# Gated DeltaNet and sparse-attention block in float32: the sparse heads' norms placed inside the DeltaNet blocks, the top-k search moved to ScalarE, masks made in parts

## The chip, the cores and the metric

The kernel runs on one core of a Trainium2 chip. The metric is the device time of one execution in microseconds (us). Before the change three runs gave 1915.55, 1920.68 and 1921.23 us; their median is 1920.68 us.

## The reference, cut to what matters

One layer over 1024 tokens of width 1024, all in float32. A projection `h @ w_in` feeds two mixers. A is a gated DeltaNet (4 heads of 128, chunks of 64 tokens). B is a sparse attention (8 heads of 64), in which an indexer's score picks 256 keys per query:

```python
dots = einsum('bqhd,bsd->bqhs', qib, ki) * (IDX_HD ** -0.5)
score = einsum('bqh,bqhs->bqs', wib, relu(dots))
score = where(admissible, score, -inf)         # whole chunks of 64, up to the query's own
_, sel = top_k(score, 256)
...
q, k = rms_norm(q per head of 64, g_q), rms_norm(k per head of 64, g_k)
logits = q.k * (DSA_HD ** -0.5) - slopes * abs(qpos - sel)      # only the selected keys
out_B = softmax(logits) @ v
...
S_t = a_t (I - b_t k_t k_t^T) S_{t-1} + b_t k_t v_t^T ;  o_t = S_t^T q_t
out_A = rms_norm(o, g_gdn_out) * silu(z)
x += concat(out_A, out_B) @ w_out ;  x += CrossAttn(...) ;  x += SwiGLU(...)
```

## The kernel before

Every engine has its own program, and semaphores join them; the order of the work is written out by hand. The stages are:

1. Norm of x, the small projections, the indexer: `score` (128 x 4608, eight tiles of 128 queries, tile t with 128(t+1) keys) is summed on VectorE.
2. Projections of the DeltaNet's q, k, v: 12 units of 128 columns (slots u). A unit is 48 matmuls on TensorE (L397 to L399) into one of two pairs of PSUM banks. ScalarE copies it out (L1427, L1428), VectorE makes the causal convolution (L1736, L1738), and ScalarE the silu (L1418).
3. 16 more units (slots v): z, and the sparse heads' q, k, v. ScalarE copies each to `cacc` (L1450) and stores it in DRAM (L1454). Beside them run the squares (L1458) and column sums (L964) of the DeltaNet's q and k, one square root (L1461), and in the last four slots their scaling (L976 on TensorE, L1760 on VectorE).
4. The DeltaNet. `gdn_order` (L571) interleaves, on every engine alike, the 16 parts of `PREP` for block b+1 (four chunks of 64 tokens) with the recurrent scan of the four chunks of block b. A block's triangular inverse takes the parts y1, z1, ... y5, z5: TensorE makes y (L1035), ScalarE copies it to `Ym` (L1484), TensorE makes zt and z (L1035), VectorE subtracts them from `TTm` (L1836) and `Tm` (L1842), and GpSimd prepares the next `gam` (L795). In the text, the body of a block is its y and z parts; its head is what comes before y1 (transposes of k and v, nkbd, kdec, vb, the decays, Am, QKm). TT5 is the last subtraction from TTm; after it follow the w matmuls (L1055). The scan of a chunk: TensorE v (L1070, L1077), ScalarE `vn` (L1528), TensorE L1091 and L1095, VectorE the state `S` (L1854), GpSimd `Sl` (L803).
5. The last four chunks (12 to 15) have no block to prepare beside them. There `dsa` puts the norm of the sparse heads: the stored q and k come back (4 MB), are squared on ScalarE (L1520), summed on TensorE (L1106), a reciprocal of 128x512 is taken (L1889), and for 16 halves of a unit TensorE spreads the factor (L1115) and VectorE scales (L1894). Then the engines meet; TensorE transposes v (L1126) and o (L1135), VectorE makes y (L1906); they meet again.
6. The sparse attention (first logits on TensorE, L1148), the output projection, the cross attention, the feed-forward part.

The top-k is a search on VectorE, 32 rounds for each of the tile pairs (7,2), (6,3), (5,4). A round takes the 8 largest of each row and overwrites them:

```python
dve.max(top8[:, 8 * k:8 * k + 8], score[:, EOFF[t]:EOFF[t + 1]]).then_inc(topk, 1)
dve.match_replace(s, top8[:, 8 * k:8 * k + 8], s, TAKEN).then_inc(topk, 1)
```

The 96 rounds stand, by `top_rounds(n)`, two in each slot u, three in each of 14 slots v, one behind each z part (and behind two parts of the head) in the blocks, and four in stage 5. `logit_bias` (L1868) turns the marked scores into a mask plus distance bias, again in stage 5.

## Time and profile before

| what | value |
| --- | --- |
| median of 3 runs | 1920.68 us |
| the profiled execution's own time | 1923.81 us |
| its span on the core | 1922.1 us |
| busy: TensorE, VectorE, GpSimd, ScalarE | 94%, 55%, 37%, 27% |
| mean granted TensorE clock | 0.965 |
| chain that ended last, by engine | TensorE 76%, VectorE 15%, ScalarE 3%, issue 3% |

Times in the trace count from the span's start. A row of the timeline gives start, length, engine, line, operation, what it writes and reads, and in brackets how long the engine stood idle ahead of it and what ended that. "PEclk" is the granted TensorE clock as a share of 2.4 GHz; 0.50 is the lower of its two levels, 1.2 GHz.

### The profile page before, as it was taken

Reading aid. Unit: us, or ns where it says so; the run is one execution under the profiler, and the core shown is the slowest. Engines: PE = TensorE matmul, PEld = TensorE weight load, DVE = VectorE, ACT = ScalarE, POOL = GpSimd, SP = SyncE. Lnnn points to the kernel's source line nnn. Section 1 sums busy time; section 2 is a strip of 40 time slices with the busy share of each in tenths; the row PEclk is TensorE's granted clock in tenths of the full one; section 3 lists DMA queues with packets and bytes.
Section 4 is the critical chain, followed back from the end, with each engine's and each line's share of the span. In section 5 each row is a group of like instructions: output and inputs, shape, how many; then the busy total and the mean of one; then the engine's idle time right before and its main releaser. Section 6 shows DMA issues by size and latency. Waiting matters only on the chain.

```text
span 1922.1 us, 28223 instructions
## 1 busy us (share of the span) xinstructions
PE 1805.2 (94%) x11097; PEld 1452.5 (76%) x11097; DVE 1059.9 (55%) x1751; ACT 513.1 (27%) x1034; POOL 716.4 (37%) x444
## 2 busy tenths in 40 slices
PE   6999999999977777799999999999999999999999
PEld 5888788777766666356787777788888888888887
DVE  4299889999858778656656347222213221322133
ACT  5366531111111123266504654100110010001000
POOL 4322233333343331056345215434244334443431
PEclk9999999999988888789999999999999999999999
DMA  7221011222220003000221000111111111111112
GB/s 227 74 59 34 23 45 52 69 85 85 94 89 2 2 2 133 12 1 2 88 66 55 23 22 25 53 55 44 44 55 46 53 44 55 44 45 53 44 44 87
DMA packets 112032, 102.42 MB, mean 53 GB/s; under 512 B 5131, under 2 KB 99390, under 8 KB 111678
## 3 DMA queue, kind: packets, MB, share of 16 engines
q1 hardware_dynamic: 109630, 92.67, 15.7%
q10 hardware_dynamic: 2304, 8.39, 1.1%
q8 instruction: 68, 1.11, 0.2%
q14 instruction: 30, 0.25, 0.0%
HBM read 87.42 MB, written 13.63 MB: 53 GB/s over the span
## 4 chain that ended last, share of the span: by engine, by line
PE 76%; DVE 15%; issue 3%; ACT 3%; SPq 1%; POOL 1%; DMA 0%; DVEq 0%; ACTq 0%
PE ps L1317 8%; PE ps L1319 8%; PE ps L1318 8%; PE ps L425 6%; PE ps L426 6%; PE ps L427 6%; PE ps L397 4%; PE ps L398 4%; PE ps L399 4%; DVE top L1723 3%; DVE cacc L1738 2%; DVE score L1727 2%; PE ps L937 2%; PE ps L1148 2%; PE ps L1173 2%
## 5 line engine op out<-in xcount | busy, mean ns | idle before, releaser
L716 POOL TENSOR_TENSOR WS<-WR,zero 128x1024 fp32r<-128x1024 f32 (+1 forms) x119 | 227.9, 1915 | 896.1 <-PE ps L399 314.9
L718 POOL TENSOR_TENSOR WS<-WR,WS 128x1024 fp32r<-128x1024 f32 (+1 forms) x119 | 300.3, 2523 | 9.4
L1317 PE MATMUL ps<-HS,WS 128*128 128x512 f32 x704 | 274.7, 390 | 3.2 <-DVE HS L333 3.2
L1319 PE MATMUL ps<-HS,WS 128*128 128x512 f32 x704 | 274.3, 390 | 0.0
L1318 PE MATMUL ps<-HS,WS 128*128 128x512 f32 x704 | 274.3, 390 | 0.0
L444 DVE TENSOR_TENSOR X<-X,ps 128x512 f32<-128x512 f32 x272 | 184.7, 688 | 155.8 <-PE ps L427 155.8
L2023 DVE TENSOR_TENSOR prod<-sil,ps 128x512 f32<-128x512 f32 x44 | 30.3, 688 | 394.7 <-PE ps L1319 394.7
L397 PE MATMUL ps<-HS,WS 128*128 128x512 f32 (+2 forms) x592 | 228.6, 386 | 7.5 <-ACT raw L1428 3.9
L398 PE MATMUL ps<-HS,WS 128*128 128x512 f32 (+2 forms) x592 | 225.5, 381 | 0.0
L399 PE MATMUL ps<-HS,WS 128*128 128x512 f32 (+2 forms) x592 | 225.1, 380 | 0.0
L1727 DVE MATCH_REPLACE8 score<-top,score 128x1024 f32<-128x1024 f32 (+2 forms) x192 | 166.9, 878 | 0.0
L1723 DVE MAX8 top<-score 128x8 f32<-128x1024 f32 (+2 forms) x192 | 161.3, 882 | 0.0
L1317 PEld LDWEIGHTS ps<-HS,WS 128*128 128x128 f32 x704 | 132.4, 188 | 31.1 <-DVE HS L333 3.8
L1319 PEld LDWEIGHTS ps<-HS,WS 128*128 128x128 f32 x704 | 132.3, 188 | 27.6
L1318 PEld LDWEIGHTS ps<-HS,WS 128*128 128x128 f32 x704 | 132.3, 188 | 27.3
L397 PEld LDWEIGHTS ps<-HS,WS 128*128 128x128 f32 (+1 forms) x592 | 111.8, 189 | 38.4 <-issue 17.2
L426 PE MATMUL ps<-WS,AS 128*128 128x512 f32 x352 | 137.0, 389 | 0.0
L427 PE MATMUL ps<-WS,AS 128*128 128x512 f32 x352 | 136.9, 389 | 0.0
L425 PE MATMUL ps<-WS,AS 128*128 128x512 f32 x352 | 136.9, 389 | 0.0
L1643 ACT ACTIVATE sil<-ps 128x512 f32<-128x512 f32 x44 | 26.4, 599 | 395.0 <-PE ps L1319 395.0
L399 PEld LDWEIGHTS ps<-HS,WS 128*128 128x128 f32 (+1 forms) x592 | 111.7, 189 | 22.1
L398 PEld LDWEIGHTS ps<-HS,WS 128*128 128x128 f32 (+1 forms) x592 | 111.9, 189 | 20.8
(282 smaller groups left out, 2894.5 us busy)
## 6 DMA issues: line engine op xcount, KB each, us to landing
WR<-in_w_gu SPq DMA_DIRECT2D x44, 512.0 KB, 3.8
WR<-in_w_in SPq DMA_DIRECT2D x36, 512.0 KB, 3.7
WR<-in_w_down SPq DMA_DIRECT2D x22, 512.0 KB, 3.6
X<-in_x SPq DMA_DIRECT2D x8, 1024.0 KB, 7.7
dsa_spill<-cacc ACTq DMA_DIRECT2D x12, 512.0 KB, 2.6
KW<-in_w_xkv SPq DMA_DIRECT2D x8, 512.0 KB, 4.9
WR<-in_w_out SPq DMA_DIRECT2D x8, 512.0 KB, 3.5
out<-X SPq DMA_DIRECT2D x8, 512.0 KB, 2.6
```

Of the source, the lines that this page charges most:

```text
L397: pe.matmul(acc, lo, src[:, 0, k, c:c + w], start=(k == 0), stop=False)
L398: pe.matmul(acc, hi, src[:, 1, k, c:c + w], start=False, stop=False)
L399: mm = pe.matmul(acc, hi, src[:, 0, k, c:c + w], start=False, stop=(k == KT - 1))
L425: pe.matmul(acc, xlo, whi, start=(s == 0), stop=False)
L426: pe.matmul(acc, xhi, wlo, start=False, stop=False)
L427: mm = pe.matmul(acc, xhi, whi, start=False, stop=(s == 1))
L716: pool.tensor_tensor(hi, w, bc(zero1[:, 0:1], [P, cols]), ALU.add).then_inc(w_hi, 1)
L718: pool.tensor_tensor(lo, w, hi.bitcast(F32), ALU.subtract).then_inc(w_split, 1)
L1317: pe.matmul(ps[:, b0 + half, :], lo, HS[:, 0, k, c], start=(k == 0), stop=False)
L1318: pe.matmul(ps[:, b0 + half, :], hi, HS[:, 1, k, c], start=False, stop=False)
L1319: mm = pe.matmul(ps[:, b0 + half, :], hi, HS[:, 0, k, c], start=False, stop=(k == KT - 1))
L1723: dve.max(top8[:, 8 * k:8 * k + 8], score[:, EOFF[t]:EOFF[t + 1]]).then_inc(topk, 1)
```

## The change

- **Search.** The 32 bits of each row's 256th largest score are now found one by one. ScalarE makes a Sign of (candidate - score) over a tile with the row sum accumulated (`counts`), VectorE compares three of these sums with a limit and sets or clears the bit (`rank`, three tiny instructions). A half step is three tiles: (7, 2, 3) or (6, 5, 4). 64 half steps: two in each slot u, three in each of the slots v = 0 to 11, four in slot 12. All rounds of max and match_replace are gone.
- **Masks.** From the found threshold VectorE makes each tile's mask (count above, ties, a running sum of the ties, two combinations, the bias); the table `MASKS` and `tail` put the pieces behind parts of the blocks and into the last four chunks.
- **Norms of the sparse heads.** The 4 MB are no longer loaded at once: units of 512 KB are loaded, squared and summed beside the y1 to z4 parts of blocks 0 and 2, loaded again, scaled and stored beside those of blocks 1 and 3 (`beside`; four units each time). The statistics use one PSUM bank; there are two square roots and two reciprocals in place of one. At the end q and k are loaded once more, already scaled.
- **End of the DeltaNet.** v is transposed in chunk 12 and o in chunks 14 and 15 (`tail`), and one meeting of the engines is gone.
- Three weight units are split on GpSimd later (their memory serves the units above).

```diff
-        DSA_PARTS = {0: ("top", 0, 0), 1: ("top", 0, 0), 2: ("on", 0, 0), 3: ("sq", 0, 8), 4: ("sq", 8, 16),
-                     5: ("sd", 0, 0), 6: ("bc", 0, 8), 7: ("bc", 8, 16)}
+        FIRST_HALF, SD_AT = 5, 14
+        def half_of(p):
+            b, i = p // len(PREP), p % len(PREP) - FIRST_HALF
+            return 8 * (b // 2) + i if 0 <= i < 8 else None
...
+            def counts(h, beside):
+                k, g = h // 2, h % 2
+                act.wait_ge(rank_cand, max(1, h))
+                for q in range(3 * g, 3 * g + 3):
+                    t, m = RANKED[q], 6 * k + q
+                    n = (t + 1) * P
+                    if m >= 2:
+                        act.wait_ge(rank_count, m - 1)
+                    act.activation((beside if m % 2 else gB)[:, 0:n], score[:, EOFF[t]:EOFF[t + 1]], ACT.Sign,
+                                   bias=cand[:, q:q + 1].bitcast(F32), scale=-1.0,
+                                   accum_out=count[:, q:q + 1]).then_inc(rank_count, 1)
...
+            def beside(p):                                  # TensorE
+                b, e = p // len(PREP), half_of(p)
+                if e is None:
+                    return
+                g, j = e % 4, e % 8 // 4
+                if b % 2 == 0:
+                    ga.wait(pe, "e1", b)
+                    d0a.wait(pe, f"sq{e}")
+                    d0p.mark(pe.matmul(ps[32 * g:32 * g + 32, 3, :], blkw[:, 30 - 2 * j:62 - 2 * j], sqh[:, e % 2, :],
+                                       start=(j == 0), stop=(j == 1), skip_group_check=True), f"st{e}")
+                else:
+                    ga.wait(pe, "e1", b)
+                    d0d.wait(pe, f"n{e - 1}" if e % 8 else f"rs{b // 2}")
+                    for hp in range(2):
+                        mm = pe.matmul(ps[SD * hp:SD * (hp + 1), 3, :], bc(pick(g, 2 * j + hp), [32, SD]),
+                                       rsH[32 * g:32 * g + 32, :], start=True, stop=True)
+                    d0p.mark(mm, f"bc{e}")
...
-                top_rounds(2)
+                for h in half_steps(u):
+                    rank(h)
...
+            MASKS = {15: [(4, "tie"), (4, "scan"), (4, "out")], 16: [(4, "bias")],
+                     22: [(3, "tie")], 31: [(3, "scan")], 32: [(3, "out"), (3, "bias")],
+                     47: [(5, "tie"), (5, "scan"), (5, "out")], 48: [(5, "bias")],
+                     54: [(2, "tie")], 56: [(2, "scan")], 58: [(2, "out")], 60: [(2, "bias")],
+                     63: [(6, "tie"), (6, "scan"), (6, "out"), (6, "bias")]}
...
+            def tail(h):                                    # VectorE
+                if h == 0:
+                    sp_.wait(dve, "o", 11)
+                    gp.wait(dve, "w1", 3)
+                    mask(7, "tie", tieT, orderT)
+                elif h == 2:
+                    scale_o(0, 0, T_ON)
+                elif h == 3:
+                    mask(7, "scan", tieT, orderT)
+                elif h == 5:
+                    mask(7, "out", tieT, orderT)
+                    dve.wait_ge(z_in, 16)
+                    dve.wait_ge(v_tr, TT)
+                    for t in range(3):
+                        y_of_tile(t)
+                elif h == 7:
+                    mask(7, "bias", tieT, orderT)
+                    for t in range(2):
+                        bias_only(t)
+                    for t in range(3, T_ON):
+                        y_of_tile(t)
```

**TensorE, block 2, parts y1 to z2** (the same in block 0 but for the scan's rows). `gam` and `TTm` make y; `Ym` and `Tm` make zt and z; vn, S are the scan. In the changed program `TTm`, `kdec`, `QKm` and others are slices of `blk`. Before:

```order
L1035 MATMUL ps<-TTm,gam 64x64 x16
L1091 MATMUL ps<-vn,kdec 128x128 x4
L1095 MATMUL ps<-vn,QKm 64x128 x4
L1035 MATMUL ps<-Ym,Tm 64x64 x16
L1035 MATMUL ps<-Tm,Ym 64x64 x16
L1035 MATMUL ps<-TTm,gam 64x64 x16
```

Changed:

```order
L1102 MATMUL ps<-blk,gam 64x64 x16
L1179 MATMUL ps<-sqh,blkw 32x512
L1162 MATMUL ps<-vn,blk 128x128 x4
L1166 MATMUL ps<-vn,blk 64x128 x4
L1102 MATMUL ps<-Ym,Tm 64x64 x16
L1102 MATMUL ps<-Tm,Ym 64x64 x16
L1179 MATMUL ps<-sqh,blkw 32x512
L1102 MATMUL ps<-blk,gam 64x64 x16
```

A column sum (L1179, `sqh` is ScalarE's square) now stands behind each y and each z, ahead of the scan's matmuls and of the next y. In blocks 1 and 3 the two matmuls of a spread factor (`ps<-rsH,ident`) stand in these places.

**VectorE, end of block 0 and begin of block 1.** Before:

```order
L1836 TENSOR_TENSOR TTm<-TTm,ps 128x512
L1723 MAX top_65<-score 128x8 x2
L1727 MATCH_REPLACE score<-top_65,score 128x768
L1727 MATCH_REPLACE score<-top_65,score 128x640
L1802 TENSOR_TENSOR nkbd<-ps,nbed 128x512
```

Changed:

```order
L1997 TENSOR_TENSOR blk<-blk,ps 128x512
L2049 RECIPROCAL rsH<-sdH 128x512
L1851 TENSOR_SCALAR orderW,count<-score,kth 128x640
L1873 TENSOR_SCALAR count<-count 128x1
L1874 TENSOR_SCALAR tieW<-score,kth 128x640
L1876 SCALAR_TENSOR_TENSOR orderW<-ones_61,tieW 128x640
L1878 SCALAR_TENSOR_TENSOR tieW<-orderW,count,tieW 128x640
L1879 SCALAR_TENSOR_TENSOR tieW<-score,kth,tieW 128x640
L1967 TENSOR_TENSOR nkbd<-ps,nbed 128x512
```

Between the block's last subtraction and the first product of the next block a reciprocal and six mask instructions have taken the place of one search round. (L1876 is the running sum.) The same stands between blocks 2 and 3 with 768 columns.

**TensorE, the last chunks up to the first logits** (`kD,qD`). Before:

```order
L1106 MATMUL ps<-sqh,blkw 32x512 x8
L1091 MATMUL ps<-vn,kdec 128x128 x4
L1095 MATMUL ps<-vn,QKm 64x128 x4
L1070 MATMUL ps<-vb,TTm 64x128 x4
L1077 MATMUL ps<-S,wTt 64x128 x4
L1084 MATMUL ps<-S,qdec 64x128 x4
L1115 MATMUL ps<-rsH,ident 64x512 x16
L1091 MATMUL ps<-vn,kdec 128x128 x4
L1095 MATMUL ps<-vn,QKm 64x128 x4
L1115 MATMUL ps<-rsH,ident 64x512 x16
L1126 MATMUL ps<-ident,vraw 128x128 x32
L1135 MATMUL ps<-ident,QKV 128x64 x64
```

Changed:

```order
L1203 MATMUL ps<-ident,QKV 128x64 x24
L1141 MATMUL ps<-blk 64x128 x4
L1148 MATMUL ps<-S,blk 64x128 x4
L1155 MATMUL ps<-S,blk 64x128 x4
L1162 MATMUL ps<-vn,blk 128x128 x4
L1166 MATMUL ps<-vn,blk 64x128 x4
L1203 MATMUL ps<-ident,QKV 128x64 x40
```

The sums and the spread factors are gone from here, the v transposes (L1193, 16 and 16) stand in chunk 12, and only 40 of the 64 o transposes are left behind the last scan matmuls.

## Rows read from the trace of the kernel before

**Rows 1.** By stretch: length, busy PE, PEld, DVE, ACT, POOL, PEclk, DMA share, GB/s.
```profile
549.00:750.00 201.00, 155.85 (x2912) 136.33 (x2912) 149.07 (x246) 39.45 (x107) 73.37 (x61) 0.86 0.05 15
...
373.00:376.00 3.00, 0.00 (x0) 0.00 (x0) 3.00 (x5) 1.94 (x3) 2.92 (x2) 0.94 0.00 0
376.00:382.00 6.00, 5.65 (x13) 4.46 (x14) 5.89 (x12) 1.29 (x3) 2.20 (x1) 0.50 0.79 262
```

**Rows 2.** Timeline of VectorE, two slots u (start us, length, instruction, idle before).
```profile
358.04 0.75 DVE L1736 TENSOR_SCALAR cacc<-raw,cols_t 128x1024 f32<-128x1024 f32 x1
...
369.29 0.74 DVE L1736 TENSOR_SCALAR cacc<-raw,cols_t 128x1024 f32<-128x1024 f32 x1
```

**Rows 3.** Timeline of ScalarE, end of the slots u and a slot v.
```profile
374.03 1.06 ACT L1418 ACTIVATE QKV<-cacc 128x1024 f32<-128x1024 f32 x1 [10.18 <-DVE cacc L1738]
...
521.03 1.08 ACT L1450 ACTIVATE cacc<-ps 128x512 f32<-128x512 f32 x2 [11.09 <-PE ps L399]
```

**Rows 4.** Groups of ScalarE by form: busy us, mean ns of one.
```profile
L1553 ACT ACTIVATE L<-L,sm 128x1024 f32<-128x1024 f32 x8 | 9.2, 1144 | 3.2 <-DVE sm L1917 3.1
...
L1553 ACT ACTIVATE L<-L,sm 128x384 f32<-128x384 f32 x8 | 4.8, 607 | 0.9 <-DVE sm L1917 0.9
```

**Rows 5.** Chain that ended last, block 1: start us, us, what.
```profile
628.05 0.69 DVE S L1854
...
641.98 0.61 DVE TTm L1836
```

**Rows 6.** Timeline of TensorE, block 1 and the end of the DeltaNet.
```profile
625.39 0.71 PE L1091 MATMUL ps<-vn,kdec 64*128 64x128 f32 x8
...
639.50 1.10 PE L1035 MATMUL ps<-Ym,Tm 64*64 64x64 f32 x32
...
766.55 1.56 PE L1106 MATMUL ps<-sqh,blkw 128*32 128x512 f32 x4 [0.20 <-ACT sqh L1520]
...
794.75 2.01 PE L1115 MATMUL ps<-rsH,ident 32*64 32x512 f32 x16
...
802.49 6.28 PE L1126 MATMUL ps<-ident,vraw 128*128 128x128 f32 x32 [0.89 <-DVEq L279]
...
815.29 0.80 PE L1148 MATMUL ps<-kD,qD 64*128 64x128 f32 x4 [0.89 <-DVEq L279]
```

**Rows 7.** Timeline of VectorE, block 0, block 1, and the last chunks.
```profile
584.78 0.68 DVE L1836 TENSOR_TENSOR TTm<-TTm,ps 128x512 f32<-128x512 f32 x1
...
589.28 0.68 DVE L1836 TENSOR_TENSOR TTm<-TTm,ps 128x512 f32<-128x512 f32 x1
...
596.57 0.69 DVE L1802 TENSOR_TENSOR nkbd<-ps,nbed 128x512 f32<-128x512 f32 x1 [3.29 <-PE ps L999]
...
747.05 0.68 DVE L1836 TENSOR_TENSOR TTm<-TTm,ps 128x512 f32<-128x512 f32 x1
...
765.11 3.43 DVE L1866 TENSOR_TENSOR QKV<-QKV,gtmp 128x1536 f32<-128x1536 f32 x2
...
777.38 0.69 DVE L1875 TENSOR_SCALAR score<-score 128x1024 f32<-128x1024 f32 x1
778.11 1.23 DVE L1876 TENSOR_TENSOR score<-score,negdist 128x1024 f32<-128x1024 f32 x1
...
782.35 3.35 DVE L1889 RECIPROCAL rsH<-sdH 128x512 f32<-128x512 f32 x1 [0.83 <-ACT sdH L1523]
```

**Rows 8.** Timeline of ScalarE, the last chunks.
```profile
759.88 1.28 ACT L1507 ACT_TABLE_LOAD   x1
761.17 0.32 ACT L1507 ACTIVATE gtmp<-ss,eps_t 128x24 f32<-128x24 f32 x1
...
765.87 1.15 ACT L1520 ACTIVATE sqh<-kD 128x512 f32<-128x512 f32 x2 [0.61 <-PE ps L1106]
```

**Rows 9.** DMA issues, 540 to 830 us: KB each, us from issue to landing.
```profile
zS<-z_spill SPq DMA_DIRECT2D x1, 2048.0 KB, 18.2
dsa_spill<-cacc ACTq DMA_DIRECT2D x1, 512.0 KB, 2.6
```

More of the change, by code:

```diff
@@ L17 @@
 F32R = mybir.dt.float32r
+I32 = mybir.dt.int32
 ALU = mybir.AluOpType
@@ L649, in _, with spill_of, load_unit, store_unit @@
             sp.dma_start(vraw[:, :, :], back[2]).then_inc(qk_in[2], 16)
+            def spill_of(u):
+                return d_dram[4 + u if u < 4 else u - 4]
+            def load_unit(u):
+                sp.dma_start(unit[:, u % 2, :], spill_of(u)).then_inc(unit_in[u % 2], 16)
+            def store_unit(u):
+                d0d.wait(sp, f"n{2 * u + 1}")
+                sp.dma_start(spill_of(u), unit[:, u % 2, :]).then_inc(unit_out[u % 2], 16)
+            for first in (0, 4):
+                for u in range(first, first + 4):
+                    if u >= first + 2:
+                        d0a.wait(sp, f"sq{2 * u - 3}")
+                    elif first:
+                        sp.wait_ge(unit_out[u % 2], 16 * 2)
+                    load_unit(u)
+                for u in range(first, first + 4):
+                    if u < first + 2:
+                        d0a.wait(sp, f"sq{2 * u + 5}")
+                    else:
+                        sp.wait_ge(unit_out[u % 2], 16 * (u // 2))
+                    load_unit(u)
+                    if u > first:
+                        store_unit(u - 1)
+                store_unit(first + 3)
+            for i in range(2):
+                sp.wait_ge(unit_out[i], 16 * 4)
             gp.wait(sp, "w1", 3)
@@ L655, in _ @@
             sp.dma_start(gB[:, :], g_xattn[0:1, :].to_broadcast([P, D])).then_inc(gB_in, 16)
+            for n in range(N_OUT + RING, N_OUT + 2 * RING):
+                load(n)
             sp.wait_ge(lg, 2 * len(duos))
@@ L1050, in prep @@
                     gd.wait(pe, "TT5", b)
+                    if b % 2:
+                        d0d.wait(pe, f"n{8 * (b // 2) + 7}")
+                    else:
+                        d0a.wait(pe, f"sd{b // 2}")
                     for ul in range(8):
@@ L1125, in _, with values_tr, o_tr @@
+            def values_tr(t):
+                if t >= 4:
+                    pe.wait_ge(v_ev, t - 3)
                 for a in range(4):
[L1126 removed]
+                    mm = pe.transpose(ps[:, t % 4, a * P:(a + 1) * P], vraw[:, a, t * P:(t + 1) * P], ident[:, :])
                 mm.then_inc(v_tr, 1)
[L1128 to L1129 removed]
+            def o_tr(t):
+                td.wait(pe, "on01" if t < T_ON else "on11")
@@ L1464, in _ @@
                     g0a.mark(act.activation(lastb[:, :], ps[:, 5, 64:128], ACT.Exp), "last")
+                if v < Z_SLOTS:
+                    for h in half_steps(12 + v):
+                        counts(h, rankA)
             for s in spilled:
@@ L1774, in _ @@
                                                       ALU.mult), "nbed")
-                if v >= 11:
-                    unit_norms(4 * (v - 11))
+                for h in half_steps(12 + v):
+                    rank(h)
+            for e0 in (0, 4, 8):
+                unit_norms(e0)
             unit_norms(12)
@@ L1906, in _, with beside @@
                 td.mark(dve.scalar_tensor_tensor(y, o, gO, z, ALU.mult, ALU.mult), f"y{t}")
+            def beside(p):
+                if p == 0:
+                    kth_flushed()
+                    above(7, orderW)
+                    above(2, orderW)
+                elif p == 3:
+                    above(3, orderW)
+                    above(6, orderW)
+                elif p == 4:
+                    above(5, orderW)
+                    above(4, orderW)
+                    kth_settled()
+                b, e = p // len(PREP), half_of(p)
+                if b % 2 == 0 and p % len(PREP) == 15:
+                    d0a.wait(dve, f"sd{b // 2}")
+                    d0d.mark(dve.reciprocal(rsH[:, :], sdH[:, :]), f"rs{b // 2}")
+                elif b % 2 and e is not None:
+                    u, src = half_unit(e)
+                    if e % 2 == 0:
+                        dve.wait_ge(unit_in[u % 2], 16 * (2 * b + u % 4 // 2 + 1))
+                    d0p.wait(dve, f"bc{e}")
+                    d0d.mark(dve.scalar_tensor_tensor(src, src, gK if u < 4 else cols_t[:, 52 + u:53 + u], ps[:, 3, :],
+                                                      ALU.mult, ALU.mult), f"n{e}")
+                for t, stage in MASKS.get(p, ()):
+                    mask(t, stage, tieW, orderW)
+                if p == 63:
+                    dve.sem_inc(masks_made, 1)
@@ L1907, in _ @@
+            gdn_order(prep, scan_v, scan_s, beside, tail)
+            scale_o(1, T_ON, TT)
+            for t in range(T_ON, TT):
+                y_of_tile(t)
             meet(2, dve)
```

296 lines of the change are left out of this document (161 added, 135 removed).

## The prediction

> **What bounds the kernel now.** I read the stretches first, then the chain of waits, then the timeline of each engine where they pointed. Projections, output projection and feed-forward are TensorE's, which is busy nearly all the time there; the change can gain in them only where TensorE stands still. It does once: for the whole of 373 to 376 it runs nothing, and for the next 6 us its granted clock is 0.50, 1.2 GHz [rows 1]. The cause stands on the other engines: a slot of VectorE, convolution and two search rounds, takes 369.29 - 358.04 = 11.25 us [rows 2], a little more than TensorE's unit, so VectorE falls behind slot by slot, the last silu waits 10.18 us for it [rows 3], and the banks behind that silu come free late. In the DeltaNet (201 us) TensorE is busy for 156 us and VectorE for 149 [rows 1]: neither is full, and the chain hops between TensorE, ScalarE, VectorE and GpSimd. From the last block's TT5 at 747.05 to the first logits at 815.29 are 68.2 us [rows 6, 7], of which four scan chunks need little: the rest is norm work, search rounds, transposes and two meetings in a line.
>
> **Projections.** Without the rounds VectorE's slot falls to under 5 us, and ScalarE has the silu ready before the banks are wanted. The stall goes: 3.6 us of standing (the empty window and its rims) and about 3.5 us for the half clock (6 to 7 us at half speed), together **-7.1** [rows 1]. What comes instead lies on ScalarE. No row shows a Sign with a sum, but the softmax's Exp has the same form (a bias per partition, a row sum): 1144 ns for 1024 columns, 607 for 384, so 0.84 ns a column on a base of 0.285 [rows 4]. A half step (1920 or 2304 columns, three instructions) is 2.5 or 2.8 us; lower bound the 1.06 of a plain activation [rows 3] per 1024, upper bound 0.2 us more each if the reading of the sum is not overlapped. In a slot u two half steps, a silu and the copies make 7.5 us. In a slot v, which TensorE sets at 1.08 + 11.09 = 12.2 us [rows 3], they are three half steps (7.9), the copy and store 1.5 and a square 1.06: 10.5 us, covered. Slot 12 has four half steps, 12.0 us; the first scaling of the DeltaNet's norms now stands behind rank() of that slot, and TensorE waits for it before its next unit: 1 us, and then at the pace of the four scalings, **+2.1** in all. If the cover breaks, see rival C. The three weight units that GpSimd splits later cost nothing: before the blocks it only gets freer, two of them follow its last Sl while VectorE still has masks and y to do, and the third stands between the Sl of chunks 13 and 14, beside a mask piece (its price is in the upper end below).
>
> **Bodies of the blocks.** Removing the rounds gains less than they last, since they mostly fill waits. In block 1 S starts at 628.05 though its matmul ended at 625.39 + 0.71: 1.95 us lost, and GpSimd's Sl and the next gam are late by it; TT5 starts at 641.98 though zt ended at 639.50 + 1.10: 1.4 us [rows 5, 6]; with smaller ones 3.6 us a body. In blocks 1 and 3 a spread factor costs TensorE 2.01/4 = 0.5 us [rows 6]. Four of the eight lie in the wait for `Ym`, four ahead of a y: +2.0. So **-1.6 each, -3.2**. In blocks 0 and 2 a column sum costs 1.56/2, in steady pace 0.88 us [rows 6]; behind y it also waits for `Ym` and then a square (0.57) [rows 8], with the scan's matmuls, which filled that wait, held behind it: 2.05 us, four times, and 0.9 four times behind z. That is +11.8 - 3.6 = 8.2 in block 2 at the present mixture of clocks; with every piece at 2.4 GHz I get 4.9. I take **+6.5**, nearer the middle since TensorE gets denser but still waits in each step. In block 0 a step of 589.28 - 584.78 = 4.5 us [rows 7] is a chain through a round; the new chain y, Ym, square, sum, zt, z, sum is 6.1, less what the first and last step gain: between +3.3 and +6.8, taken **+5**.
>
> **Heads.** TT5 ends at 589.96 and nkbd can start at 596.57: 6.6 us free on VectorE [rows 7]. Now the reciprocal needs 3.35, and starts 0.3 after TT5 (the square root behind a table load). The mask pieces of 640 columns, by 0.69 and 1.23 us per 1024, are 0.49 + 0.1 + 0.49 + 3 x 0.83 + gaps = 3.7 us; of 768 columns 4.2 [rows 7]. So nkbd is 0.8 (block 1) and 0.9 (block 3) late. The first Exp after the square root loads a table, 1.28 us [rows 8]; 0.6 of it is hidden by the copy of S, 0.7 remains. Together **+3.1**. Block 2's head takes masks of 512 columns in idle time: nothing.
>
> Two rules of the Trainium skill speak against me here. The row shows a table load of 1.28 us from 759.88 and the next activation at 761.17, directly behind it [rows 8]. "ScalarE: Activation LUTs", section "What ACT_TABLE_LOAD costs", adds a drain of about 1.38 us to every switch; by it the two heads would cost 2.8 us more. No row shows a running sum; I price it like a two-input operation and hold twice that possible. "DVE: opcode table, instruction layouts, handler registers and perf-mode slots", section "Datapath and trigger behaviour", says that this program runs at half throughput; by it the heads and the end together would cost about 3.5 us more.
>
> **The end.** From TT5 of block 3 to the logits the longest engine is now VectorE: the mask of tile 6 (0.63 twice, 1.08 four times, 0.1: 5.7), of tile 7 (6.4), the scaling of o (3.43, 1.3 and the reciprocals: 5.2), four states of 0.7 (2.8), the plain biases (1.4), eight tiles of y, taken like the 0.68 of another 512-column instruction out of PSUM (5.6): 27.1 us [rows 7]. To this come waits that nothing fills: about 2.7 us in each of three scan chunks (v, vn, L1091), the square root with its load 1.6 [rows 8], the last chunk's sum and root, the last transposes and the meeting 4: 13.7, so 40.8 us. TensorE (half of the 6.28 us of v transposes ahead of a state) and ScalarE (eight copies) fit in. z lands 18.2 us after its issue [rows 9], and its first use is near 28. So **-27.4** against 68.2; between -20 (each mask instruction at the two-input price, half clock in every chunk, and GpSimd late with Sl behind its weight split) and -33.
>
> **Sum.** -7.1 + 2.1 - 3.2 + 6.5 + 5 + 3.1 - 27.4 = -21.0 us. The profiled execution took 1923.81, which gives 1902.8; the median of the runs is 3.1 lower, so I name **1900**. A measurement of this kernel can tell about 0.3%, 5.8 us, from no change: under 1914.9 is faster, over 1926.5 slower.
>
> **Rivals.** A: the blocks give back more. Each unit goes round through DRAM: store and load, 2.6 us each at the size of 512 KB [rows 9], with issue and semaphores near 6.5, between the scaling of its bank's last owner and its own, three parts later (6 to 8 us). If VectorE waits at four such places 1.5 us in each odd block, and the even bodies take their upper ends (+3.5), and the clock stays as low as 0.86 [rows 1], the sum is -21.0 + 4 x 1.5 x 2 + 3.5 = -5.5: **1915**, on the bound of "same". For it: every engine's order is strict, a late unit stops the whole chain. Against: stores run on an idle queue. One half of it gives 1907. B: more gain. The denser blocks hold 2.4 GHz; of 201 us a clock of 0.86 means some 56 us at half, and where TensorE is the chain up to 8 us come back: **1892**. C, the other side: ScalarE becomes the bound of the slots v. Its spare there is 12.2 - 10.5 = 1.7 us for nine counts. With x us more per count each of 13 slots grows by 9x - 1.7; at x = 0.36 the whole gain is gone, at x = 0.5 the slots grow by 36 us: **1936**. For it: each count waits for a candidate and for its bank's sum, and no Sign is in the trace. Against: the Exp row has the same form and waits. D: the search is hidden either way and the end does not shrink, since VectorE's 27 us wait behind GpSimd and each other: -7 there only, with all else as forecast: 20 us less gained, **1920**.
>
> **Numbers.** Forecast (1892 to 1909) 0.50, A 0.20 (three quarters of it faster), B 0.13, D 0.07, C 0.08, others 0.02. Range **1884 to 1921**: it takes B with its lower bound of the end and reaches to D, and leaves out C. Faster 0.81, same 0.11, slower 0.08.
>
> **What would show it.** Right: no empty window on TensorE near 374; ScalarE's Sign of 1024 columns near 1.14 us; nkbd of blocks 1 and 3 some 7.5 us behind TT5; y to zt in block 2 near 3 us with a square and a sum between them; bodies of blocks 0 and 2 longer than those of 1 and 3; 38 to 45 us from the last TT5 to the first logits. Wrong: TensorE waiting for `cacc` in the slots v (C), VectorE waiting for DMA at the scalings (A), a clock near 1.0 in the DeltaNet (B), or an end of over 55 us (D).

## The result and the profile after

The changed kernel is slower. Its median is 1932.95 us over 8 runs (1924.05 to 1934.28) against 1920.75 over 8 runs of the kernel before (1915.55 to 1924.53): a ratio of 1.0058, 95% interval 1.0038 to 1.0078, 12 us. The forecast was 1900 with a range of 1884 to 1921. The profiled execution of the changed kernel took 1933.25 us, span 1931.4; the one before 1923.81, span 1922.1. Six of the changed kernel's eight runs took 1932.5 to 1934.3 us at a mean granted clock of 0.965 to 0.968, the profiled one among them, and two took 1924 and 1926 us at 0.975 and 0.973. The spans differ by 9.3 us. The table shows where the difference lies. TT0 is the first write of a block's TTm, ahead of y1; nkbd is the first product of a block's head:

| stretch | before | after | difference | forecast |
|---|---|---|---|---|
| start to nkbd of block 0 | 550.05 | 550.63 | +0.6 | -5.0 |
| nkbd to TT0, four blocks | 61.1 | 64.0 | +2.9 | +1.4 |
| TT0 to TT5, blocks 0 / 1 / 2 / 3 | 25.3 / 29.6 / 27.9 / 30.0 | 32.6 / 35.1 / 37.9 / 32.4 | +7.3 +5.5 +9.9 +2.4 | +5 -1.6 +6.5 -1.6 |
| TT5 to the next nkbd, three heads | 7.3 / 7.6 / 8.2 | 9.8 / 8.1 / 11.1 | +5.9 | +1.7 |
| last TT5 to the first logits | 68.2 | 44.7 | -23.5 | -27.4 |
| first logits to the end | 1106.8 | 1105.2 | -1.6 | 0 |

The +3.1 that the prediction gives the heads is split here: 0.8 and 0.9 for a late nkbd, and twice 0.7 for the table load of the first Exp, which runs behind nkbd (at 617.63, where nkbd is at 608.61). The four blocks and their heads took 33.9 us more, where 11.4 were forecast, and the lead of the projections did not arrive.

Stretches of the changed kernel (columns as in [rows 1]):

```profile
373.00:376.00 3.00, 3.00 (x15) 2.50 (x14) 0.00 (x0) 2.08 (x4) 2.63 (x2) 1.00 0.30 120
376.00:382.00 6.00, 6.00 (x28) 4.99 (x27) 0.99 (x6) 6.00 (x15) 1.68 (x1) 1.00 0.39 116
515.00:533.00 18.00, 17.06 (x60) 11.98 (x60) 5.12 (x9) 0.81 (x2) 0.00 (x0) 0.81 0.08 30
549.00:782.00 233.00, 189.70 (x2976) 141.28 (x2976) 113.77 (x160) 53.90 (x128) 72.39 (x60) 0.86 0.19 65
```

The hole of [rows 1] at 373 to 376 is filled, at a granted clock of 1.00, and in the next 6 us the granted clock is 1.00 in place of 0.50. In the DeltaNet VectorE is busy for 114 us of 233 and TensorE for 190, against 149 and 156 of 201 before: the load moved to TensorE, at the same clock of 0.86.

Groups of ScalarE by form, the counts of the search (mean ns is the third number):

```profile
L1509 ACT ACTIVATE gB<-score,cand 128x1024 f32<-128x1024 f32 x32 | 36.6, 1143 | 3.9 <-DVE cand L1846 1.6 <-DVE cand L1826 1.2 <-ACT cacc L1549 0.9
L1509 ACT ACTIVATE rankA<-score,cand 128x384 f32<-128x384 f32 x20 | 12.0, 602 | 0.0
```

A Sign with its sum costs what the Exp of [rows 4] costs (1144 and 607). The search fits its cover: the slot from 502.55 to 514.73 takes 12.18 us, and the same slot before (508.86 to 521.03) took 12.17, so rival C is out. It goes wrong just behind the search. ScalarE, TensorE and VectorE around slot 12 (three timelines, one fence each):

```profile
514.73 1.09 ACT L1549 ACTIVATE cacc<-ps 128x512 f32<-128x512 f32 x2
...
533.02 1.09 ACT L1549 ACTIVATE cacc<-ps 128x512 f32<-128x512 f32 x2 [17.21 <-PE ps L409]
```

```profile
502.45 1.14 PE L1043 MATMUL ps<-rsT,ident 32*128 32x512 f32 x8
...
514.30 0.39 PE L409 MATMUL ps<-HS,WS 128*128 128x512 f32 x1
515.94 3.77 PE L1043 MATMUL ps<-rsT,ident 32*128 32x512 f32 x8 [1.25 <-DVE QKV L1924]
519.64 0.80 PE L407 MATMUL ps<-HS,WS 128*128 128x512 f32 x1
520.23 0.63 PE L408 MATMUL ps<-HS,WS 128*128 128x512 f32 x1
```

```profile
515.11 4.39 DVE L1924 SCALAR_TENSOR_TENSOR QKV<-QKV,ps 128x512 f32<-128x512 f32 x7
```

At 514.73 the kernel is 6.3 us ahead of before (521.03 in [rows 3]). The next copy comes at 533.02, where before it came at 533.21: TensorE stood 1.25 us for the first scaling, went through four spread factors at the scalings' pace (3.77 where the group before took 1.14), and came back with a matmul each 0.43 us in place of 0.23. Ten matmuls ran at that pace, at a granted clock of 0.50 (519.7 to 524), and 2.1 us were lost by it; the wait and the slow factors had taken 1.25 + 3.77 - 1.14 = 3.9.

VectorE's TT in the steady steps of block 0, and the head of block 1:

```profile
587.61 0.69 DVE L1997 TENSOR_TENSOR blk<-blk,ps 128x512 f32<-128x512 f32 x1 [4.77 <-PE ps L1102]
...
594.00 0.69 DVE L1997 TENSOR_TENSOR blk<-blk,ps 128x512 f32<-128x512 f32 x1 [4.77 <-PE ps L1102]
...
598.83 0.69 DVE L1997 TENSOR_TENSOR blk<-blk,ps 128x512 f32<-128x512 f32 x1 [3.21 <-PE ps L1102]
599.61 3.35 DVE L2049 RECIPROCAL rsH<-sdH 128x512 f32<-128x512 f32 x1
...
603.89 1.31 DVE L1874 TENSOR_SCALAR tieW<-score,kth 128x640 f32<-128x640 f32 x1
605.24 1.49 DVE L1876 TENSOR_TENSOR_SCAN orderW<-ones,tieW 128x640 f32<-128x640 f32 x1
...
608.61 0.69 DVE L1967 TENSOR_TENSOR nkbd<-ps,nbed 128x512 f32<-128x512 f32 x1
```

A step takes 6.39 us where it took 4.50 [rows 7]; VectorE stands 4.77 us of each for TensorE. And one step of TensorE in block 0, then a factor of block 3:

```profile
582.03 1.04 PE L1179 MATMUL ps<-sqh,blkw 128*32 128x512 f32 x2
583.01 1.15 PE L1102 MATMUL ps<-blk,gam 64*64 64x64 f32 x32
585.46 1.02 PE L1179 MATMUL ps<-sqh,blkw 128*32 128x512 f32 x2 [1.31 <-ACT sqh L1624]
586.41 1.15 PE L1102 MATMUL ps<-Ym,Tm 64*64 64x64 f32 x32
...
757.58 1.07 PE L1185 MATMUL ps<-rsH,ident 32*64 32x512 f32 x4
```

y, then 1.31 us of nothing (Ym and the square behind it on ScalarE), the sum, zt, z, the next sum. A sum alone costs 1.0 us, a factor alone 1.07, both at a granted clock of 1.00.

### The profile page after: what moved, and what is told of

The parts are those of the page before. It is cut to its first block, busy times and chain, and to the rows that moved or that the text cites. A ratio compares the mean times of both kernels' runs of the same rounds, so it can differ in the third digit from the quotient of the medians.

```text
span 1931.4 us, 28422 instructions
## 1 busy us (share of the span) xinstructions
PE 1811.4 (94%) x11097; PEld 1450.3 (75%) x11097; DVE 853.8 (44%) x1427; ACT 682.8 (35%) x1423; POOL 721.7 (37%) x444
## 4 chain that ended last, share of the span: by engine, by line
PE 55%; DVE 4%; issue 1%; POOL 1%; ACT 1%; DVEq 0%; POOLq 0%; ACTq 0%
PE ps L1401 8%; PE ps L1402 8%; PE ps L1403 8%; PE ps L435 6%; PE ps L437 6%; PE ps L436 6%; PE ps L1232 2%; PE ps L1257 2%; PE ps L1243 2%; PE ps L1314 1%; PE ps L1102 1%; PE ps L1335 1%; PE ps L1352 1%; PE ps L1354 1%; PE ps L1353 1%
## 5 line engine op out<-in xcount | busy, mean ns | idle before, releaser
L1753 ACT ACTIVATE sil<-ps 128x512 f32<-128x512 f32 x44 | 26.3, 598 | 395.0 <-PE ps L1403 394.9
L1403 PEld LDWEIGHTS ps<-HS,WS 128*128 128x128 f32 x704 | 132.2, 188 | 27.4
L1816 DVE SCALAR_TENSOR_TENSOR score<-relu,wba,score 128x512 f32<-128x512 f32 (+3 forms) x150 | 104.6, 755 | 13.3 <-ACT relu L1497 11.9
L1758 ACT ACTIVATE AS<-prod 128x512 fp32r<-128x512 f32 x44 | 27.8, 632 | 230.1 <-DVE prod L2204 230.1
```

The costliest lines, as they stand in the source:

```text
L1403: mm = pe.matmul(ps[:, b0 + half, :], hi, HS[:, 0, k, c], start=False, stop=(k == KT - 1))
```

## The experiments

Three kernels leave something out and give prices. The theory (called N in the texts) was that TensorE's sums and factors and their waits, standing in the order of the blocks, took the 34 us; the rivals were the mask pieces on VectorE (M), and that the rounds had been hidden anyway (C0). "Stretch" below is first nkbd to last TT5, "end" last TT5 to first logits, and "head" with a time is TT5 to the next nkbd. Two cautions hold for all runs. The sizes are read from one trace of each version. The medians of the kernel before, measured beside each group of runs, lie between 1918.3 and 1921.4 us, so a difference of whole kernels of different groups is good to some 3 us: by the ratios to before, run 4 gains 13.6 us on the changed kernel, by the medians 17.1, by the stages of its trace 17.6.

**1. No norms beside the blocks.** `beside` of TensorE and ScalarE, VectorE's reciprocals and scalings and the units' loads and stores are taken out of the changed kernel.

> The changed kernel without the head norms beside the blocks: squares, column sums, square roots, reciprocals, spread factors, scalings and the units' way through DRAM are left out, so q and k of the sparse attention stay unscaled. From the first nkbd to the last TT5 the changed kernel takes 230.9 us (before: 197.0). Theory N (the 34 us more are TensorE's column sums of 1.04 us and spread factors of 1.07 us in the order of its blocks, and the waits for the squares): the stretch falls to 190 to 200 us, and the whole kernel to some 1895. Rival M (the mask pieces on VectorE, in the heads and bodies, hold the chain): it stays over 215. Rival G (with the rounds gone nothing was gained, and TensorE's half clock stretches whatever is there): the stretch falls by under 15 us.

Measured: 1881.81 us, stretch 731.46 - 549.31 = 182.15, end 44.7, unchanged.

```profile
549.31 0.69 DVE L1941 TENSOR_TENSOR nkbd<-ps,nbed 128x512 f32<-128x512 f32 x1 [1.46 <-PE ps L1061]
...
731.46 0.69 DVE L1971 TENSOR_TENSOR blk<-blk,ps 128x512 f32<-128x512 f32 x1 [0.77 <-PE ps L1097]
```

The norms cost 48.7 us in the stretch: 11.0, 9.9, 12.2 and 6.6 in the bodies of blocks 0 to 3, 2.9, 1.8 and 3.4 in the heads, 1.0 ahead of TT0. Both results are lower than N gave (190 to 200, and 1895). That the norms hold the stretch is shown. The run takes them out whole, so it does not say how much of it is TensorE's own sums and factors, and how much the waits for squares, scalings and units.

**2. No mask pieces** of tiles 2 to 6 (`MASKS = {}`).

> The changed kernel without the mask pieces beside the blocks and ahead of the last chunks: tiles 2 to 6 keep their raw scores in place of the mask, only tile 7's is made. Theory N: the heads of blocks 1 and 3 lose 2.5 to 3 us each and the bodies nothing, so the stretch from the first nkbd to the last TT5 goes from 230.9 to about 225; the end (44.7 us) loses the 5.7 us of tile 6. Whole kernel about 1921. Rival M: the stretch falls below 212.

Measured: 1924.38 us; stretch 222.64, which is 8.3 us less, 3.5 and 2.5 of it in the heads of blocks 1 and 3; end 45.8. M is out. Block 3's body is 3.0 us longer than in the changed kernel; its first step takes 9.52 us at a granted clock of 0.58, in place of 7.61 at 0.78. What I did not expect is the end: 5.7 us of VectorE's work of tile 6 less, and nothing gained. That work runs beside w and chunk 12.

**3. The kernel before without the rounds** beside and behind the blocks (all `top_rounds` behind the projections taken out).

> The kernel before without the search rounds beside the blocks and behind them: only those of the projections are made, so the masks come from a search that is not finished. The prediction priced the rounds at 3.6 us a body. By it the bodies of blocks 1 to 3 (TT0 to TT5: 29.6, 27.9, 30.0 us) fall to 26, and the stretch from the first nkbd to the last TT5 from 197.0 to 185 to 187. Rival C0 (the rounds only filled waits of the chain, and TensorE, or GpSimd's gam, sets the step): the bodies fall by under 1.5 us each, the stretch stays over 192; then 11 us of the prediction's working never were there.

Measured: 1900.24 us. Stretch 179.17, bodies 22.3, 24.5, 24.8, 24.5: 3.0, 5.1, 3.2 and 5.4 less. The 3.6 us a body of the prediction were right, if anything small. So the change in the stretch is -17.8 for the rounds, +48.7 for the norms and +3.0 for the rest (182.15 against 179.17).

The next kernels move one thing each.

**4. The square ahead of Ym** on ScalarE:

```diff
 def prep(b, part):                                   # ScalarE
+    e = half_of(len(PREP) * b + PREP.index(part))
+    if b % 2 == 0 and e is not None:
+        ...
+        d0a.mark(act.activation(sqh[:, e % 2, :], src, ACT.Square), f"sq{e}")
...
 def beside(p):
-    ...
-        d0a.mark(act.activation(sqh[:, e % 2, :], src, ACT.Square), f"sq{e}")
```

> The changed kernel with one order changed: in blocks 0 and 2 ScalarE makes the square of a half unit ahead of the copy Ym of the same part, not behind it, so that the column sum can run in TensorE's wait for Ym. Theory N: the wait of 1.31 us ahead of each of the eight sums behind a y goes, and so does the second part of the wait for Ym: bodies of blocks 0 and 2 (32.6 and 37.9 us) lose 5 to 8 us each, the kernel some 12, to about 1921. Rival W (TensorE's own work sets these bodies, the wait would be filled by nothing): under 2 us a body, and the kernel within 4 us of 1933.

Measured: 1915.85 us, 17.1 less than the changed kernel, 0.9987 of before (0.9976 to 0.9998). Its TensorE in block 0:

```profile
578.79 1.15 PE L1102 MATMUL ps<-blk,gam 64*64 64x64 f32 x32
579.87 1.04 PE L1179 MATMUL ps<-sqh,blkw 128*32 128x512 f32 x2
580.84 1.15 PE L1102 MATMUL ps<-Ym,Tm 64*64 64x64 f32 x32
```

The sum fills the wait for Ym, and TensorE does not stand still there. A step is 5.04 us, the bodies of blocks 0 and 2 are 26.3 and 31.8, so 6.3 and 6.1 less. Rival W is out.

**5. The first four scalings inside slot 12:**

```diff
-                for h in half_steps(12 + v):
-                    rank(h)
-            for e0 in (0, 4, 8):
-                unit_norms(e0)
-            unit_norms(12)
+                for i, h in enumerate(half_steps(12 + v)):
+                    if v == 12:
+                        unit_norms(i, i + 1)
+                    rank(h)
+            unit_norms(4, 16)
```

> The changed kernel with one order changed: the first four scalings of the DeltaNet's norms stand one by one ahead of the four half steps of slot 12, not behind all of them. In the changed kernel TensorE's second group of spread factors starts at 515.94 and its next unit is 6 us late against the lead it had at 514.73; the prediction gave this wait 2.1 us. Theory S (TensorE stands for these scalings and comes back at 1.2 GHz): the first nkbd comes 5 to 6 us earlier, at 545 (550.63), and the kernel takes about 1927. Rival S0 (the lead is lost to something else there, the stores or the meeting ahead of the blocks): nkbd stays within 1.5 us.

Measured: 1926.91 us, 6.0 less.

```profile
512.16 1.09 ACT L1549 ACTIVATE cacc<-ps 128x512 f32<-128x512 f32 x2
...
524.34 1.09 ACT L1549 ACTIVATE cacc<-ps 128x512 f32<-128x512 f32 x2 [11.09 <-PE ps L409]
```

The slot takes 12.18 us, at a granted clock of 1.00, where the changed kernel took 533.02 - 514.73 = 18.29: 6.1 us, three times what the prediction gave. (This execution was 2.6 us earlier already ahead of slot 12, so its nkbd at 541.50 is 9.1 earlier.)

**6. All masks in the bodies**, tile 7's too, by another table: tile 7 and the first pieces of tile 6 behind steps of block 0, the rest of 6 and half of 3 in block 1, 3, 5, 4 and a piece of 2 in block 2, the rest of 2 in block 3.

> The changed kernel with all mask pieces, those of tile 7 too, put behind steps of the bodies, where VectorE is idle for 4.8 us a step in blocks 0 and 2 and 1.8 us in blocks 1 and 3; none is left in a head or in the end. Theory N: bodies stay within 1 us each, the heads of blocks 1 and 3 (9.78 and 11.08 us) fall to 8 or less, the end (44.7 us) to 32 to 38 since 7 us of tile 7 no longer stand between the chunks; kernel 1915 to 1920. Rival M: pieces beside GpSimd's work hold the steps, bodies grow by 2 us or more each, and the kernel gains under 5 us.

Measured: 1920.69 us, 12.3 less. Heads of blocks 1 and 3 at 6.2 and 8.2; end 38.7; bodies of blocks 0 to 2 within 0.3, block 3 at 38.0 (32.4). The 6 us of the end came from tile 7 alone (compare run 2), since its pieces stood between the chunks and ahead of y. The expectation of bodies within 1 us failed in block 3: its fourth step, where a piece stands, takes 8.96 us against 6.70, and its first 9.52 at a granted clock of 0.58 against 7.61 at 0.78.

**7. The reciprocal moved** behind the part gq of blocks 1 and 3, the square root one part earlier (`SD_AT` is 13, and `if b % 2 and p % len(PREP) == 1` ahead of it).

> The changed kernel with the reciprocal of the norms (3.35 us) moved from the heads of blocks 1 and 3 behind their first part, into VectorE's idle time ahead of Am, and the square root one part earlier, ahead of the last TT. If the heads are long because VectorE carries reciprocal and masks one behind the other, they fall from 9.78 and 11.08 to 7 to 8 us, and TensorE's wait of 0.94 and 1.64 us for the root ahead of w goes; kernel 1926 to 1929. If the table load and TensorE's half clock make them long, they stay over 9.

Measured: 1920.61 us, 12.3 less, more than expected. The heads fall to 6.9, 6.3 and 7.9: 7.8 us. The stretches from nkbd to TT0 are 2.8 us shorter together, and block 1's body 4.3. The last is mostly TensorE's clock. Stretch of the first step of block 1, TT0 to the next TT, in the changed kernel and in this one:

```profile
625.79:635.32 9.53, 7.83 (x90) 5.88 (x92) 2.13 (x4) 0.98 (x2) 3.63 (x4) 0.55 0.01 3
```

```profile
621.64:627.70 6.06, 4.36 (x92) 3.36 (x94) 2.03 (x4) 0.98 (x2) 2.31 (x3) 1.00 0.01 4
```

The same 92 matmuls take 3.5 us less, at a granted clock of 1.00 in place of 0.55. From TT5 to TT0 it is 621.64 - 599.88 = 21.8 us against 27.0, and the granted clock from nkbd to TT0 is 0.98 against 0.80. Block 3 goes the other way: its first step takes 9.16 us at 0.63 in place of 7.61 at 0.78, and its body is 1.6 us longer. A low clock in a block's first step did not come with the change. It stood there before:

```profile
612.29:618.63 6.34, 5.52 (x88) 5.21 (x90) 4.67 (x9) 0.98 (x2) 2.05 (x3) 0.55 0.00 0
717.09:723.83 6.74, 5.93 (x86) 5.61 (x88) 4.66 (x9) 0.98 (x2) 2.45 (x3) 0.50 0.01 2
```

These are the first steps of blocks 1 and 3 in the kernel before. From version to version this clock lies between 0.50 and 1.00 and goes with 1.5 to 3.5 us of a body, so a smaller difference in one of these bodies, read from one trace, says little.

**8. All four edits together**, with GpSimd's three weight splits also moved, from the end into the first steps of the sparse attention.

> The changed kernel with the square ahead of Ym, the scalings in slot 12, all masks in the bodies, the reciprocal moved, and also GpSimd's three weight splits moved from the end into the first steps of the sparse attention. The parts lie in stages of their own, so their gains should add: -17 (measured for the square) - 5.5 - 10 to -15 - 3, and some 3 more for the splits, which doubled VectorE's times in the end: 1890 to 1898, with the end at 28 to 34 us. If they overlap, over 1905.

Measured: 1905.24 us (0.992 of before, 0.9901 to 0.9939), end 35.8. The gains did not all add: the bodies of blocks 1 and 3 are 36.4 and 36.6, where run 4 has 32.4. VectorE in block 1:

```profile
619.93 0.75 DVE L2049 SCALAR_TENSOR_TENSOR unit<-unit,cols_t,ps 128x512 f32<-128x512 f32 x1 [1.40 <-PE ps L1180]
620.60 1.15 DVE L1872 SCALAR_TENSOR_TENSOR tieW<-orderW,count,tieW 128x896 f32<-128x896 f32 x1
621.78 1.15 DVE L1873 SCALAR_TENSOR_TENSOR tieW<-score,kth,tieW 128x896 f32<-128x896 f32 x1
622.97 0.69 DVE L1991 TENSOR_TENSOR blk<-blk,ps 128x512 f32<-128x512 f32 x1
```

No idle time stands ahead of TT, so the piece is on the chain.

**9. The pieces out of the bodies of blocks 1 and 3**, again by the table alone.

> The kernel with all four edits and late weight splits (1905.2 us), with the mask pieces taken out of the bodies of blocks 1 and 3, where steps of 8.97 and 10.53 us stood against 6.7 without them, and put in the bodies of blocks 0 and 2, the head of block 2, its wait for GQ, and behind the last TT5. Theory N (VectorE has room in the even blocks' steps only; in the odd ones it carries two scalings a step): bodies of blocks 1 and 3 fall from 36.4 and 36.6 to 31 to 32.5, the others keep theirs, and the kernel takes 1896 to 1899. If TensorE's half clock made those steps long, nothing changes: over 1903.

Measured: 1897.42 us (0.988, 0.9862 to 0.9898), as N forecast for the kernel. The bodies are 33.9 and 35.2, better by 2.5 and 1.5 only, and not the 31 to 32.5 expected. The fourth steps fell from 8.97 and 10.53 to 6.71, but the first ones stand at 8.40 and 9.52 us, at a granted clock of 0.69 and 0.56.

Then the price of a sum and of a factor. In [rows 6] 16 records took 2.01 us, and I divided by four factors. The changed kernel's factor of 1.07 us has 4 records. Either it is dear alone, or the four overlapped. The window of that row in the kernel before shows one thing more, which the prediction did not use:

```profile
794.75:796.76 2.01, 2.01 (x18) 0.33 (x16) 0.00 (x0) 1.83 (x10) 0.00 (x0) 0.50 0.00 0
```

The granted clock was 0.50. Four factors took 2.01 us at half speed, and one alone takes 1.07 at full speed, which is nearly the same number of clocks.

**10. Two sums in a row** behind y, none behind z, on top of run 4 (`for e in (e, e + 1) if e % 2 == 0 else ():` around square and sum).

> The kernel with the square ahead of Ym (1915.85 us), with the two column sums of a step one directly behind the other, in the wait for Ym, and none behind z. The two write different 32 partitions of the bank. In the trace of before four records in such a row took 1.56 us [two sums], where one sum alone takes 1.02 to 1.05 in the changed kernel. Theory L (TensorE works on them side by side when they stand in a row, and alone each costs its full length): bodies of blocks 0 and 2 (26.3 and 31.8 us) lose 2 to 4 us each, the kernel 4 to 8. Rival: the pair costs 2.1 and fills the wait no better, bodies change by under 1 us.

Measured: 1914.07 us. The row of two sums:

```profile
580.75 1.05 PE L1180 MATMUL ps<-sqh,blkw 128*32 128x512 f32 x4
```

Four records take 1.05 us, where two took 1.04 in run 4, so the second sum adds nothing here. Steps of block 0 fall from 5.04 to 4.09, bodies of blocks 0 and 2 from 26.3 and 31.8 to 22.8 and 29.6. The whole kernel gains 1.8 us by the medians, less than the 5.7 of these bodies and less than the 4 to 8 expected: the heads behind these bodies grew by 0.8, 1.6 and 0.2, the end from 44.7 to 47.2, and block 3's body by 1.6, which block 1's gives back.

**11. Two factors in a row** behind y, on top of run 4; the second goes into bank 2, and z waits for its scaling.

> The kernel with the square ahead of Ym (1915.85 us), with the two spread factors of a step one directly behind the other, behind y, the second into the bank that z leaves free, and both scalings behind them. Before, 16 records in a row took 2.01 us [four factors, 0.50 each]; in the changed kernel one factor alone takes 1.07. Theory L: the pair takes 1.1 to 1.3 us in place of 2 x 1.07 with a wait for a scaling between, in the wait for Ym, so the bodies of blocks 1 and 3 (32.4 us both) fall by 3 to 5 us each, to 28 or so; kernel 1906 to 1910. Rival: two factors in a row take 2.1 us, under 1.5 us a body.

```profile
640.07 1.09 PE L1192 MATMUL ps<-rsH,ident 32*64 32x512 f32 x8
```

Eight records in 1.09 us: again side by side. But the kernel takes 1915.93 us, as run 4, where 1906 to 1910 were expected. Block 1's body falls from 32.4 to 30.0, of which 1.5 us are its first step at a granted clock of 1.00 in place of 0.78. Block 3's stays at 32.6, where its first step is 9.54 us at 0.55 against 7.63 at 0.78. In the four later steps the pairs give back 0.9 and 1.7 us. The size of the overlap is shown; a gain of the kernel by itself is not.

**12. Run 9 with both pairs.**

> The kernel of the first run of this group (masks in the even blocks) with paired sums and paired factors as well. If all add: 1897 - 6 - 8 = 1883, within 5 us; over 1892 would say that the pieces hide in each other's waits.

Measured: 1889.54 us (0.9842, 0.9825 to 0.986). Stretch 742.39 - 542.59 = 199.8, end 33.9. The pairs are worth 7.9 us here of the 14 expected.

**13. The weight splits alone** moved into the attention, for the forecast's missing 4 us of the end.

> The changed kernel with only GpSimd's three weight splits moved, from beside tile 7's mask pieces and y into the first steps of the sparse attention. In the end of the changed kernel VectorE's instructions of 1024 columns take 2.20, 3.24 and 2.01 us beside a split (1.23 is the price the prediction took), two plain copies 2.58, and Sl 2.02 and 2.96 (1.04 alone). If the two engines get in each other's way, the end falls from 44.7 to 38 to 41 us, and these instructions to 1.2 to 1.3; the steps of the attention lose some of it again, so the kernel takes 1928 to 1931. If the end is set by the chain of the chunks and VectorE's slow instructions are hidden, it stays over 43.

VectorE and GpSimd in the end of the changed kernel, then VectorE in this run:

```profile
803.90 2.20 DVE L1878 SCALAR_TENSOR_TENSOR tieT<-orderT,count,tieT 128x1024 f32<-128x1024 f32 x1
806.13 3.24 DVE L1879 SCALAR_TENSOR_TENSOR tieT<-score,kth,tieT 128x1024 f32<-128x1024 f32 x1
```

```profile
800.21 2.96 POOL L860 TENSOR_TENSOR Sl<-S,lastb 128x512 f32<-128x512 f32 x1 [6.12 <-DVE S L2014]
803.13 1.89 POOL L773 TENSOR_TENSOR WS<-WR,zero 128x1024 fp32r<-128x1024 f32 x1
805.09 3.20 POOL L775 TENSOR_TENSOR WS<-WR,WS 128x1024 fp32r<-128x1024 f32 x1
```

```profile
803.37 1.28 DVE L1873 SCALAR_TENSOR_TENSOR tieT<-orderT,count,tieT 128x1024 f32<-128x1024 f32 x1
804.68 1.95 DVE L1874 SCALAR_TENSOR_TENSOR tieT<-score,kth,tieT 128x1024 f32<-128x1024 f32 x1
```

The end falls from 44.7 to 39.75 us, and the kernel stays at 1932.67: behind the first logits it takes 1110.2 us in place of 1105.2. In this kernel the splits cost 5 us in either place.

**14. Run 12 with the splits back in the end**, where it has no mask of tile 6 or 7 left.

> The kernel with all edits and pairs (1889.5 us), with the three weight splits back in the end, where the changed kernel has them. The run before showed them worth nothing either way in the changed kernel: 5.0 us less in the end, the same lost behind the first logits. In this kernel no mask of tile 6 or 7 stands in the end, so the splits meet only the scalings and y there: if that is why they cost, the end grows from 33.9 by 1 to 3 us, the attention gives back 5, and the kernel takes 1885 to 1888. If the splits slow the scalings as much as they slowed the masks, 1889 to 1892.

Measured: 1885.16 us (1884.45 to 1887.64), 0.9823 of before, 0.9801 to 0.9846. The end is 37.1 us, 3.3 more, and the part behind the logits 7.7 less, 1103.1 us. This is the fastest version, 35 us under before and 48 under the change as it was made (45 by the ratios to before).

## Why the prediction was wrong

**Projections, -5.0, measured +0.6.** The stall went as described, and 6.3 us of lead stood at slot 12. Of these 0.9 are from ahead of the convolutions (238.39 to 237.54 at the first copy), so the stall gave 5.4 of the 7.1. The step that failed is "1 us, and then at the pace of the four scalings, +2.1": run 5 measured 6.1. The order of events was right and two sizes were not. The wait and the pace took 3.9 us (1.25, and 3.77 in place of 1.14). The half clock behind them took the other 2.1 (ten matmuls at 0.43 in place of 0.23), and had no term, although the same prediction had counted just that for the stall at 374.

**Bodies of blocks 1 and 3, -1.6 each, measured +5.5 and +2.4.** The step that failed is "a spread factor costs TensorE 2.01/4 = 0.5 us [rows 6]", with four of eight hidden, so +2.0 a body. Run 1 measured 9.9 and 6.6 for all that the norms put there. The row is four factors side by side at half clock, and one factor at a time, each behind the scaling of the last, costs 1.07. On paper that is 8 x 0.57 = 4.6 us a body more, and with 2.0 gives the 6.6 of block 3. The match is partly luck: in run 11, where two factors take the time of one, the four later steps give back only 0.9 and 1.7 us. How the rest divides between the price of a factor, the wait for the scaling ahead of each next one, and factors that were not hidden in the wait for `Ym` after all, stays open. In the four later steps the norms cost 7.2 and 6.3 us, nearly the same in both blocks. The difference between the blocks is in the first step, which cost 2.6 us more in block 1, at a granted clock of 0.55 with and 0.54 without the norms, and 0.3 in block 3, at 0.78 with and 0.53 without. The 3.6 us for the rounds were low (run 3: 5.1 and 5.4), which hid part of the error.

**Body of block 2, +6.5, measured +9.9.** The terms were right: 11.8 us for the sums against 12.2 (run 1), 3.6 for the round against 3.2 (run 3). Their difference is the 8.2 of my upper end. What failed is the choice of the middle "since TensorE gets denser": its granted clock there was 0.91 (before 0.94), and the sums still cost their full price. Run 4 shows that half of that price, 6.1 us, was the order of square and `Ym` on ScalarE. **Block 0, +5, measured +7.3:** the step came out at 6.39 as against 6.1, and the first, from which the working took something off, is 1.8 us longer than before (7.99 against 6.19). Only the last step gained.

**Heads, +3.1, measured +8.8,** of which 5.9 up to nkbd (1.7 forecast) and 2.9 from there to TT0 (1.4 forecast). The order of events was right: root, reciprocal, masks, nkbd. The term that failed is the 3.7 us of mask pieces, which took 5.7. The running sum of 640 columns is 1.49 us and not the 0.83 of a two-input operation. The second comparison took 1.31 in place of 0.49, beside GpSimd's instructions, and the first, which also adds up its row, 0.78. Run 7 shows that reciprocal and masks are a problem only one behind the other. The table load behind nkbd held Am for 0.61 and 0.63 us, as forecast (0.7). Of the 2.9 us 1.7 are block 0's, where runs 1 and 2 do not remove them; their cause stays open.

**The end, -27.4, measured -23.5.** The failed step is that the three weight units "cost nothing": they cost the end 5.0 us (run 13, the end at 39.75 where 40.8 were forecast). That this sum comes so near without the splits is partly luck: it added all of VectorE's work, and by runs 2 and 6 tile 6's was hidden and tile 7's was not.

**The rivals.** C (ScalarE the bound) did not come: the counts cost what the Exp does. A named the right place, "the blocks give back more". Its even bodies at their upper ends came, and its clock of 0.86 too. Its main mechanism did not: in the changed kernel VectorE waits at no scaling for a DMA. Single waits of this kind, 1.6 to 1.7 us, appear in runs 4, 7 and 9. B did not come, since the clock stayed at 0.86, nor D, since the end shrank by 23.5 us. A, B and D each kept the wrong price of the factor, so no case reached the measured time except C, whose 1936 lies near by chance. The error was in a shared input, not in the weights of the cases.

Of the two rules of the Trainium skill, the one on the running sum ("DVE: opcode table, instruction layouts, handler registers and perf-mode slots", "Datapath and trigger behaviour") agrees with the trace: 1.49, 1.76, 2.02 and 2.28 us for 640, 768, 896 and 1024 columns are 2.0 to 2.1 ns a column, and the combination, with 0.89 us for 640 and 1.28 for 1024 (run 13), takes 1.0 ns a column. Of the 3.5 us that the prediction worked out from it all but tile 6's 0.9, which run 2 shows hidden, belonged into the sum. The added drain at a table load ("ScalarE: Activation LUTs", "What ACT_TABLE_LOAD costs") is not seen: the copy ahead of the load ends at 721.20, the load of 1.28 us begins at 721.22, and the root behind it at 722.51. Here the measurement decides.

## What to carry to other kernels

A row of several instructions gives the price of the row, not of one: before dividing, ask whether the instructions could overlap there, whether they still can where they are going, and at which granted clock the row ran. Work that is put beside a chain should be made ready ahead of the wait that it is to fill (here the square ahead of Ym), or it becomes a link of it. A wait on TensorE is to be priced with the lower clock behind it, and a mask piece, a split or a reciprocal by the idle time of exactly that step and by what its neighbour engine does then.

## What was not expected of the hardware

Matmuls that stand directly in a row and use different rows or columns of the array ran side by side: two sums of 32 output partitions took 1.05 us together and 1.04 alone, two factors of 32 input partitions 1.09 together and 1.07 alone, four 1.14 (the 8 records at 502.45, with 128 outputs each), all at a granted clock of 1.00. The Trainium skill has this as a rule, "TensorEngine Tiling (Array Packing)", "Key Properties": tiles work independently, and loads and matmuls on different ones can run in parallel. The trace agrees. The other side of it is that a lone one took as long as the whole row.

VectorE and GpSimd slow each other in both directions. Combinations of 1024 columns took 2.20 and 3.24 us beside a split. In run 13, without splits, they took 1.28 and 1.95, the second beside a Sl of 2.02. Sl took 2.96 us beside VectorE's running sum of 1024 columns, in run 13 too, where no split is near, and 1.04 alone. "SBUF — State Buffer", section "SBUF: two separate sides", of the Trainium skill says that an operation of VectorE with two inputs from SBUF and one of GpSimd that reads SBUF lock each other out for the whole instruction. The lengths fit: the combination at 806.13 has 2.16 us to wait until the split ends at 808.29, and 1.08 are left of its 3.24. No run here separates the lock from a slower pace.
